# One-core transformer kernel: the expert layers' weights in 16 KB pieces and eight slots, one 128-row tile for two experts' hidden rows, and the expert loops written out

## The reference, cut to what matters

```python
def grouped_moe(x, router_w, router_bias, w_gate, w_up, w_down):   # x2: [256, 1024]
    aff = sigmoid(x2 @ router_w)                     # [256, 16]
    # best group of 4 experts, then the best 2 experts in it
    gates = ...                                      # [256, 16], two non-zero a row
    for g_e, wg_e, wu_e, wd_e in (gates.T, w_gate, w_up, w_down):
        h = silu(x2 @ wg_e) * (x2 @ wu_e)            # wg, wu: [1024, 512]
        acc = acc + (h @ wd_e) * g_e[:, None]        # wd: [512, 1024]
    return acc
x = layer_norm(ALPHA * x + grouped_moe(x, ...))
```

## Time and profile before

| | us |
|---|---|
| median of three runs | 1563.94 |
| the profiled execution, its own time | 1561.53 |
| its span, first to last instruction | 1559.8 |
| PE busy in it | 1399.9 |
| expert layer 0: first `gate_up` to the end of the last `down` | 206.3 to 451.9 |
| expert layer 1: the same | 687.7 to 935.2 |

### The profile page before, as it was taken

How to read it: one execution, slowest core, us unless ns; L and a number is a source line. 1 busy time by engine, 2 the same in 40 slices (tenths; PEclk the granted TensorE clock), 3 DMA queues, 4 the chain that set the end, 5 groups by cost and what they waited for, 6 DMA issues and landing times.

```text
span 1559.8 us, 15911 instructions
## 1 busy us (share of the span) xinstructions
PE 1399.9 (90%) x6338; PEld 903.6 (58%) x6338; DVE 428.5 (27%) x961; ACT 272.6 (17%) x598; POOL 61.5 (4%) x97
## 2 busy tenths in 40 slices
PE   7868689999979996869999997999889996999997
PEld 6654444454435774445444535876667685888743
DVE  1992311111130232221111103145522304222201
ACT  4022110010010333111000112131143403000000
POOL 4910000000000000000000000000000000000000
PEclk9979789999989995879999998998999998999999
DMA  9710259999995051329999995131223033344420
GB/s 361 230 48 18 96 201 395 396 393 393 393 393 176 0 179 65 108 74 393 393 395 396 393 393 202 54 109 54 76 86 108 1 108 108 109 161 162 162 81 27
DMA packets 146506, 307.75 MB, mean 197 GB/s; under 512 B 5634, under 2 KB 29950, under 8 KB 146447
## 3 DMA queue, kind: packets, MB, share of 16 engines
q1 hardware_dynamic: 139968, 298.85, 52.4%
q10 hardware_dynamic: 6479, 8.07, 1.6%
HBM read 305.86 MB, written 1.06 MB: 197 GB/s over the span
## 4 chain that ended last, share of the span: by engine, by line
PE 81%; DVE 11%; DMA 5%; issue 2%; ACT 1%; ACTq 0%; DVEq 0%; POOL 0%; POOLq 0%
PE psum L233 35%; PE psum L1289 13%; PE psum L1325 6%; PE psum L544 6%; PE psum L2512 5%; DMA ring<-in_moe_w_up 5%; DVE arena L878 3%; PE psum L1336 3%; PE psum L759 2%; PE psum L733 2%; PE psum L1310 2%; PE psum L425 1%; PE psum L1474 1%; PE psum L1472 1%; PE psum L2170 1%
## 5 line engine op out<-in xcount | busy, mean ns | idle before, releaser
L233 PE MATMUL psum<-xT,ring 128*128 128x256 f32 (+2 forms) x1792 | 405.4, 388 | 6.2 <-POOLq L405 5.2
L233 PEld LDWEIGHTS psum<-xT,ring 128*128 128x128 f32 x1792 | 341.4, 192 | 66.5 <-issue 11.0
L1289 PE MATMUL psum<-ring,arena 128*64 128x512 f32 x1024 | 226.2, 594 | 3.2 <-issue 1.7
L1289 PEld LDWEIGHTS psum<-ring,arena 128*64 128x64 f32 x1024 | 73.9, 137 | 138.5 <-issue 138.2
L1325 PE MATMUL psum<-ring,arena 128*64 128x512 f32 x512 | 117.7, 614 | 1.8 <-ACT arena L1250 1.8
L233 PE MATMUL psum<-arena,x_nat 128*128 128x128 f32 x512 | 69.1, 292 | 16.7 <-issue 16.7
L233 PEld LDWEIGHTS psum<-arena,x_nat 128*128 128x128 f32 x512 | 63.5, 202 | 29.1 <-issue 28.2
L1325 PEld LDWEIGHTS psum<-ring,arena 128*64 128x64 f32 x512 | 36.9, 141 | 70.5 <-issue 68.8
L1180 DVE TENSOR_TENSOR arena<-psum,arena 64x512 f32<-64x512 f32 x32 | 22.3, 695 | 200.1 <-ACT arena L1236 200.1
L2512 PE MATMUL psum<-ring,arena 128*128 128x512 f32 x176 | 75.7, 592 | 0.0
L878 DVE SCALAR_TENSOR_TENSOR arena<-arena,vec 128x256 f32<-128x256 f32 x150 | 75.0, 575 | 0.7
(11 more groups left out here) (302 smaller groups left out, 1308.5 us busy)
## 6 DMA issues: line engine op xcount, KB each, us to landing
ring<-in_moe_w_gate SPq DMA_DIRECT2D x32, 2048.0 KB, 15.8
ring<-in_moe_w_up SPq DMA_DIRECT2D x32, 2048.0 KB, 19.7
ring<-in_moe_w_down SPq DMA_DIRECT2D x32, 2048.0 KB, 15.7
ring<-in_w_in SPq DMA_DIRECT2D x11, 2048.0 KB, 15.3
ring<-in_w_up SPq DMA_DIRECT2D x22, 1024.0 KB, 7.7
ring<-in_a_w_pw SPq DMA_DIRECT2D x6, 2048.0 KB, 19.5
ring<-in_w_down SPq DMA_DIRECT2D x5, 2048.0 KB, 7.7
ring<-in_w_kv SPq DMA_DIRECT2D x4, 2048.0 KB, 19.4
```

The source lines that it names most:

```text
L233: last = nc.tensor.matmul(dst, lhsT, rhs, start=(n == 0), stop=(n == len(pairs) - 1))
L1289: last = pe.matmul(bank(j)[part, :], tokens[:, k, side * SEATS:side * SEATS + SEATS], slot_k(u + n)[:, k, :], start=(k == 0), stop=(k == K ...
```

## The change

- **Weight order.** The source of an expert's matrix is read as `(p k) n -> p k n`: a partition takes 16 KB that lie together (8 successive rows of a gate or up matrix, 4 of a down matrix). The features are then dealt out to the partitions in another order. So the tokens are gathered from a reordered copy `by_row` that ACT makes in `route` (two copies, each waited for), and the hidden columns are reordered by a strided read in `hidden`. The scaled residual, which was the separate `base`, is made in place in `x_nat`.
- **Two more slots.** Expert units go round eight slots: the ring's six, one in `arena` at 6690, and one in two halves (`arena` at 11100 and the first 2048 columns of `xT`), loaded by two DMAs. SP waits for the mixer's last projection before the seventh unit (`region_free`), and for the router product, the last reader of `xT`, before the eighth.
- **One tile for two experts.** The first expert's hidden rows lie in the lower 64 partitions, the second's in the upper 64, so `turn` is four transposes of 128 x 128.
- **Gates in the seats.** DVE writes `gated` (seat times gate) in one operation, that is what is transposed, and the product that picked each seat's gate is gone, with `gate_col`. `gatedT` is double.
- **Order on PE.** `scatter(p - 1)` stands behind `gate_up(1)`, ahead of `turn`; both fetches stand behind `turn`. ACT reads out `turn` ahead of the fetch.
- **Loops.** All eight pairs are written out on all engines and on SP.
- **Norm rows.** The loads that were issued after `constants`, `route0`, `attention` and `route1` are issued after `overflow0`, `moe0`, `overflow1` and `moe1`.

The diff, cut to its core:

```diff
-IN_PAIR = {... ("GU0", "S", "GU1", "X0", "T", "X1", "Y0", "Y1")}
+IN_PAIR = {... ("GU0", "S", "GU1", "T", "X0", "X1", "Y0", "Y1")}
...
+        if moe and moe[0] % (RING + MORE) >= RING:
+            slots.append(moe[0] % (RING + MORE))
+        elif moe:
+            slots.append((u - moe[0] + moe[0] % (RING + MORE)) % RING)
...
+    halves = arena[:, 11100:11100 + 2048], xT[:, :, :].rearrange("p c t -> p (c t)")[:, 0:2048]
...
+                if m == RING:
+                    job_ready(sp, FJ[("pw2", "att_o")[layer]] + 3)
...
+                elif m == RING + 1:
+                    job_ready(sp, FJ[f"route{layer}"])
...
-                src = src.rearrange("(k p) n -> p k n" ...)
+            src, n = a[f"moe_w_{kind}"][layer, e].rearrange("(p k) n -> p k n", p=P), D if kind == "down" else DE
+            region_free(u)
+            if slots[u] == RING + 1:
+                for half in range(2):
+                    at = half * 2048 // n
+                    load(u, src[:, at:at + 2048 // n, :], halves[half].rearrange("p (k n) -> p k n", n=n))
...
-            act.activation(base[:, :, :], x_nat[:, 1:3, :], ACT.Copy, scale=ALPHA)
+            for t in range(2):
+                act_step(act.activation(by_row[:, t, :, :], x_nat[:, t + 1, :].rearrange("p (f k) -> p k f", k=KC),
+                                        ACT.Copy))
+            act.activation(x_nat[:, 1:3, :], x_nat[:, 1:3, :], ACT.Copy, scale=ALPHA)
...
-                            [(x_nat[:, t + 1, k * P:k * P + P], sources[:, t, :]) for t in range(2)])
+                            [(by_row[:, t, k, :], sources[:, t, :]) for t in range(2)])
...
-                dve.tensor_tensor(hid[HIGH, side, :], bank(j)[HIGH, :], silu_g[HIGH, side, :],
+                by_row = lambda x: x.rearrange("s (f k) -> s k f", k=DE // P)
+                dve.tensor_tensor(hid_both[part, :].rearrange("s (k f) -> s k f", f=P), by_row(bank(j)[part, :]),
+                                  by_row(silu_g[part, 0, :]), ALU.mult)
...
-                products(bank(j)[:, 2 * P:2 * P + 2], [(seats[:, t, :], gate_cell[:, t, :]) for t in range(2)]
...
-                for side in range(2):
-                    for k in range(DE // P):
-                        last = pe.matmul(bank(j)[:, at:at + SEATS], hid[HIGH, side, k * P:k * P + P], ident[HIGH, HIGH], ...)
+                for k in range(DE // P):
+                    last = pe.transpose(bank(j)[:, k * P:k * P + P], hid_both[:, k * P:k * P + P], ident[:, :])
...
+            for p in range(PAIRS_E):
+                for j in gathers(p):
+                    read_out(pe, j)
+                gate_up(0, p)
+                turn_seats(p)
+                gate_up(1, p)
+                if p == 1:
+                    pe.wait_ge(cleared, 1)
+                if p > 0:
+                    scatter(p - 1)
+                turn(p)
+                if p < LAST:
+                    fetch(0, p + 1)
+                    fetch(1, p + 1)
+                down(p)
             scatter(LAST)
...
     next_norm = {
-        "constants": (1, ...), "route0": (2, ...), "attention": (3, ...), "route1": (4, ...),
+        "overflow0": (1, ...), "moe0": (2, ...), "overflow1": (3, ...), "moe1": (4, ...),
```

More of the change, by code:

```diff
@@ L312, in program, with weights @@
         src = units[u][0]
-        dmas = 2 if isinstance(src, tuple) and not isinstance(src[0], str) else 1
+        dmas = 2 if (isinstance(src, tuple) and not isinstance(src[0], str)) or slots[u] == RING + 1 else 1
         landed.append((landed[same[-1]] if same else 0) + 16 * dmas)
+    halves = arena[:, 11100:11100 + 2048], xT[:, :, :].rearrange("p c t -> p (c t)")[:, 0:2048]
     def slot(u):
-        return ring[:, slots[u], :]
+        return arena[:, 6690:6690 + 4096] if slots[u] == RING else ring[:, slots[u], :]
+    def weights(u, k, n=512):
+        if slots[u] == RING + 1:
+            half, k = divmod(k, 2048 // n)
+            return halves[half].rearrange("p (k n) -> p k n", n=n)[:, k, :]
+        return slot_k(u, n)[:, k, :]
     def slot_k(u, n=512):
@@ L364, in _ @@
             src = units[u][0]
[L365 to L372, removed]
             if u == 1:
@@ L1163, in _, with seat @@
         def _(dve):
[L1164 to L1169, removed]
+            def seat(p):
                 for t in range(2):
                     for side in range(2):
+                        e = 2 * p + side
@@ L1194, in gathered, with summed @@
+            def gathered(j):
+                job_ready(dve, j)
                 dve.tensor_copy(tokens[:, 4:8, :], bank(j).rearrange("p (c s) -> p c s", c=4)).then_inc(
                     bank_free[j % BANKS], 1)
-            def summed(p, i=0):
+            def summed(p):
                 j = job("Y1", p)
[L1199 to L1212, removed]
+                job_ready(dve, j)
+                dve.tensor_copy(y_pair[:, 512:D], bank(j)).then_inc(bank_free[j % BANKS], 1)
@@ L1214, in _ @@
             seat(0)
+            gate_seats(0)
             gathered(B + 1)
             dve.memset(psum[:, BANKS:2 * BANKS, :], 0.0).then_inc(cleared, 1)
[L1218 to L1221, removed]
+            for p in range(PAIRS_E):
+                if p < LAST:
+                    seat(p + 1)
+                hidden(0, p)
+                turned_seats(p)
+                hidden(1, p)
+                if p < LAST:
+                    gate_seats(p + 1)
+                    gathered(job("X1", p))
+                summed(p)
@@ L1231, in _, with silu, gathered @@
         def _(act):
-            def silu(side, p, i=0):
+            def silu(side, p):
                 j = job(f"GU{side}", p)
[L1235 to L1239, removed]
+                job_ready(act, j)
+                act.activation(silu_g[UP_IN[side], 0, :], bank(j)[GATE_IN[side], :], ACT.Silu).then_inc(silu_ready, 1)
+            def gathered(j):
+                job_ready(act, j)
@@ L1258, in _ @@
[L1258 to L1262, removed]
+            gathered(B)
+            for p in range(PAIRS_E):
+                silu(0, p)
+                silu(1, p)
+                j = job("T", p)
+                job_ready(act, j)
+                act.activation(hidT_both, bank(j).rearrange("p (k s) -> p k s", s=P), ACT.Copy).then_inc(
+                    bank_free[j % BANKS], 1)
+                if p < LAST:
+                    gathered(job("X0", p))
+                j = job("Y0", p)
+                job_ready(act, j)
+                act.activation(y_pair[:, 0:512], bank(j), ACT.Copy).then_inc(bank_free[j % BANKS], 1)
@@ L1264, in _, with free, fetch @@
         @block.tensor
         def _(pe):
[L1266 to L1273, removed]
+            def free(j):
+                pe.wait_ge(bank_free[j % BANKS], j // BANKS)
+            def fetch(half, p):
                 j = gathers(p)[half]
-                pe.wait_ge(seats_ready, p + 1 + i)
-                free(j, i)
+                pe.wait_ge(seats_ready, p + 1)
+                free(j)
@@ L1278, in fetch, with gate_up @@
                 gather(half, bank(j)).then_inc(job_done, 1)
-            def gate_up(side, p, i=0):
+            def gate_up(side, p):
                 j = job(f"GU{side}", p)
                 u = U + RING * p + 2 * side
-                free(j, i)
-                wait_unit(u, i)
-                wait_unit(u + 1, i)
+                free(j)
+                unit_ready(u)
+                unit_ready(u + 1)
                 for k in range(KC):
-                    for n, part in enumerate((LOW, HIGH)):
+                    for n, part in enumerate((GATE_IN[side], UP_IN[side])):
@@ L1323, in down @@
                     for k in range(DE // P):
                         for side, part in enumerate((LOW, HIGH)):
-                            last = pe.matmul(bank(j)[part, :], hidT[:, side, k * SEATS:k * SEATS + SEATS],
-                                             slot_k(u + side, D)[:, k, half * 512:half * 512 + 512], start=(k == 0),
+                            last = pe.matmul(bank(j)[part, :], hidT_both[:, k, side * SEATS:side * SEATS + SEATS],
+                                             weights(u + side, k, D)[:, half * 512:half * 512 + 512], start=(k == 0),
```

167 lines of the change are left out of this document (72 added, 95 removed).

## The result

The change makes the kernel 2.6% faster. The median is 1524.45 us (four runs, 1519.31 to 1528.17) against 1564.84 for the kernel before beside it; the ratio is 0.974, 95% interval 0.972 to 0.977. The forecast was 1534: right in direction, 10 us short of the gain, inside the wide range (1522 to 1549) and just outside that of the likeliest case alone (1525 to 1541). The profiled execution took 1519.31 us, the shortest of the four; its span is 42.2 us shorter than the one before.

The account below looks back on a forecast made before the run. PE was taken to bound both expert layers, transfers just behind. Layer 0's 13.1, layer 1's 14.8 and the branch's 3.0, less 1 us, took 29.9 from 1561.53; with 2.4 added for the median, 1534 us, range 1522 to 1549.

Parts of the forecast that it names:

- likeliest case: The forecast itself, without its rivals: 1525 to 1541 us around 1534, chance 0.61.
- The bound: In both expert layers PE sets the time, 30.99 us a middle pair, and the transfers stand just behind it.
- T: Transpose of the hidden rows in each pair: four 128 x 128 transposes take 0.81 us instead of 1.93, 1.12 saved.
- G: The two gathers (fetches) of a middle pair, 1.98 us each on PE; no saving was forecast from moving them.
- S: Seat piece of a pair: the gate products go, two transposes take 0.40 us instead of 0.56; 0.25 saved was taken.
- Pair 0: First pair of an expert layer: a 1.6 us wait becomes bare, so its 27.72 us change by +0.2.
- The clock's rival: Pair 0's gap lowers PE's clock, up to 3 us a layer, and the last `down` stays slow: 1544 us, chance 0.13.
- Pair 7: Last pair of a layer: covered wait and last `down` of 7.02 us; saves 4.5 us in layer 0, 5.9 in layer 1.
- Transfers: Expert weights in 16 KB pieces move 430 GB/s where 389 is needed; weight waits of 0.6 and 0.9 us go.
- The branch: PE's branch over the unused block, 5.3 and 6.5 us, ends sooner with norm rows fetched later: 1.5 us a layer.
- Route: ACT's three copies for one in `route` end by 189 or 191 us, hidden by DVE's work until 193.
- Loops: Written-out pairs cost PE no instruction more and no wait for instructions; priced at nothing.

Follow-up runs that it names:

- fetches around: The changed kernel with the two fetches around the transposes again (fetch, turn, fetch), as in the kernel before: 1516.07 us, ratio 0.971 to the kernel before.
- half rows: The changed kernel with hidden rows turned in the old form, 16 records of 64 x 64 from the upper 64 partitions: 1554.28 us, ratio 0.991.
- products: The changed kernel with hidden rows turned by four plain products with the identity instead of four transposes: 1532.09 us, ratio 0.981.

## Why the prediction was right, and where it was short

**The bound.** Right. PE bounded both layers and the transfers stood just behind: long pieces alone give nothing, the new work and order on PE alone 5 us.

**T.** The step that failed most. I took 0.20 a transpose from L425's busy time and used the 0.11 that stood in the earlier trace rows only for the fast end of the range. A middle pair has 0.44 in all, so 1.49 is saved where I took 1.12: 0.37 x 12 = 4.4 us in the middle pairs. The row beside full streams was the right one. L425's transposes come behind waits, partly at the lower clock: 16 of them take 3.68 us at a granted clock of 0.50 (614.8 to 618.6 us).

**G.** I priced the moved fetches at nothing; they save 0.39 a pair, 4.7 us in all, since none stands behind a half-width group any more (fetches around, half rows). This is a term that the sum didn't have. A hint of it stood in the earlier trace rows: the 16 records of a fetch are 1.98 behind the half-width pieces, 0.124 each, where the two records of the seat transposes, behind a full-width group, show 0.11 each.

**S.** 0.19 saved for 0.25, the seats now standing behind a half-width group.

**Pair 0.** 27.72 became 27.56 for a forecast of 27.9. The bare wait is 1.9, not 1.6, since the strided product takes 1.07 us for 0.70. The clock's rival didn't show in the changed kernel; it did in three layers of two others (products, half rows), at 1.6 to 3.0 us each, so it was a fair risk.

**Pair 7.** 31.3 became 26.3 in layer 0, 5.0 saved for 4.5, and 32.7 became 26.3 in layer 1, 6.4 saved for 5.9. Its last `down` is 7.10 where 7.02 was forecast. That the gaps are what lowered the clock is half shown: with them back it fell in one layer of two. With the 0.9 alone no last `down` was slow.

**Transfers.** The rate was well forecast, 425 to 427 GB/s where the line gave 430. The long pieces do travel whole: with long pieces alone 69.45 MB went in 4239 packets of 8 KB or more, 16 KB each on average. The changed kernel, which loads one unit of eight in two halves, shows 4954 such packets for 72.18 MB. That the DMA share would fall below full was wrong: the pair got so short that 12.58 MB in 28.92 us ask 435 GB/s, and the queues stayed full. The rule in the Trainium skill (DMA: Bandwidth & Descriptors, Where 436 GB/s comes from) that HBM binds at about 358 GB/s a core isn't borne out by any of these stretches (393 to 427 GB/s, with one core at work). Even with 435 asked the stock lasts, with six slots nearly too. Of the two extra slots I had no price of their own; beside long pieces they are worth 0.6 us a layer, beside short ones more: 244.1 against 233.3.

**The branch.** I took 1.5 us a layer. In layer 0 the branch is 1.3 to 2.0 us shorter, by the cause I named. The stretch ahead of the experts is about 1 us shorter in six profiles with the later fetch (34.1 to 34.5 for 35.3) and 2.2 to 2.7 in four (32.6 to 33.1), whose first gathers behind the branch take 5.1 to 5.4 us where the six show 6.4 to 6.7. Layer 1 gave 4.7 to 6.1, and the norm rows don't explain it: fetched early they left its branch at 0.44. So most of this gain came by a cause that I hadn't named.

**Route.** The strided copies cost double (4.11 us for the two, where L941 took 1.90 for as many columns), and DVE's work hid them as reckoned.

**Loops.** No wait for instructions showed in the written-out pairs.

The sum for the experts was 27.9 and is 38.3: T 4.4, G 4.7, and the rest from pairs 0 and 7, less S. The stretch ahead of layer 1 adds what the branch and a lucky clock gave. The total hides this in part: the gains in the profile come to 49.9 us (38.3 in the experts, 11.6 in the two stretches ahead of them), and the other stretches, slower by 7.7, took the sum down to 42.2.

## What to carry to other kernels

Where the engine and the transfers stand level, price both: a gain on one is worth its size only up to what the other has in reserve, and each half alone measures as little or nothing (here 0 and 5 us of 40). For an operation in a full stream take its price from the nearest row of that stream, not from a group's mean over stretches that start cold. And when work is moved, look at the width of the group ahead of it, and cover each bare wait at the edges of a loop, not only in its middle.

## What the runs showed of the hardware that I had not expected

- A float32 transpose is one record and a product with the identity two: 0.44 against 0.89 for four of 128 x 128.
- A full-width group behind a half-width one costs about 0.2 us more (1.98 against 1.78; 0.37 against 0.22 for the seats).
- DVE's product over 64 x 512 with both sources read in steps of four elements takes 1.07 us, contiguous 0.70. ACT's copy in steps of eight takes twice as long.
- The same branch took 0.35 to 6.6 us on PE. With 1 MB of norm rows fetched ahead of it, it took 6.2 in place of 3.4 to 4.0 in layer 0, and 0.44 as without them in layer 1.
- Behind equal gaps the granted clock fell in one layer and not in the other of the same execution (last `down` 8.80 and 7.10 us).
